# Two scan chains in one pass: the forward states of a bidirectional state-space kernel computed in the projection

## The reference

```python
acum = cumsum(dt * a)                       # per head, inside the chunk
decay = exp(acum[l] - acum[s])              # lower triangle
y_diag = (C @ B.T * decay) @ (x * dt)       # "inside" the chunk
chunk_state = B.T @ (x * dt * exp(acum[-1] - acum))
h_next = h * exp(acum[-1]) + chunk_state    # the chain over the chunks
y_off = (C @ h) * exp(acum)                 # "offset": what the state before the chunk gives
```

## Time and profile before

| | us |
|---|---|
| median of 3 runs (lowest, highest) | 3406.49 (3401.08, 3413.98) |
| span of the profiled execution | 3403.3 |
| TensorE busy over the span | 3177.5 (93%) |
| VectorE, ScalarE, GpSimd busy | 1650.4 (48%), 966.6 (28%), 373.6 (11%) |
| state steps in the projection, first to last sum | 997 to 1143 |
| output stage of the scan, first and last matmul | 1221.5 to 1525 |

### The profile page before, as it was taken

How to read it: one execution, slowest core, us unless ns; L and a number is a source line. 1 busy time by engine, 2 the same in 40 slices (tenths; PEclk the granted TensorE clock), 3 DMA queues, 4 the chain that set the end, 5 groups by cost and what they waited for, 6 DMA issues and landing times. The chain is left out here.

```text
span 3403.3 us, 37747 instructions
## 1 busy us (share of the span) xinstructions
PE 3177.5 (93%) x14940; PEld 2520.6 (74%) x14940; DVE 1650.4 (48%) x1911; ACT 966.6 (28%) x1784; POOL 373.6 (11%) x229
## 2 busy tenths in 40 slices
PE   8999999997999969977999969999999799999898
PEld 8788888876888847766888858888877455555577
DVE  4645543475014249984444443243343555564365
ACT  4422121111210145532222231233223334433310
POOL 0000000000012136652000000000000201000012
PEclk9999999998999989998999979999999699999899
DMA  6122323432226356544333342223123412210242
GB/s 216 42 61 72 107 89 127 149 109 84 88 97 219 109 166 184 180 138 155 111 112 125 115 158 65 89 87 105 56 93 93 102 38 51 62 38 7 93 130 99
DMA packets 211149, 358.99 MB, mean 105 GB/s; under 512 B 22074, under 2 KB 143674, under 8 KB 203093
## 3 DMA queue, kind: packets, MB, share of 16 engines
q1 hardware_dynamic: 187190, 324.46, 29.6%
q10 hardware_dynamic: 16368, 26.36, 2.2%
q0 software_dynamic: 7456, 6.27, 0.9%
HBM read 235.09 MB, written 121.81 MB: 105 GB/s over the span
## 5 line engine op out<-in xcount | busy, mean ns | idle before, releaser
L668 PE MATMUL p_ps<-hmT_hi,p_w_hi 128*128 128x512 f32 x1312 | 524.1, 399 | 16.4 <-ACT p_work L372 14.1
L668 PE MATMUL p_ps<-hmT_lo,p_w_hi 128*128 128x512 f32 x1312 | 512.8, 391 | 0.0
L668 PE MATMUL p_ps<-hmT_hi,p_w_lo 128*128 128x512 f32 x1280 | 500.9, 391 | 0.0
L1795 PE MATMUL p_ps<-h2T_hi,p_w_hi 128*128 128x512 f32 x800 | 329.3, 412 | 22.1 <-DVE h2T_lo L1652 22.1
L1795 PE MATMUL p_ps<-h2T_lo,p_w_hi 128*128 128x512 f32 x800 | 315.7, 395 | 0.0
L668 PEld LDWEIGHTS p_ps<-hmT_hi,p_w_hi 128*128 128x128 f32 x1312 | 247.8, 189 | 71.4 <-issue 18.6
L1795 PE MATMUL p_ps<-h2T_hi,p_w_lo 128*128 128x512 f32 x768 | 300.4, 391 | 0.0
L668 PEld LDWEIGHTS p_ps<-hmT_lo,p_w_hi 128*128 128x128 f32 x1312 | 248.0, 189 | 49.8
L668 PEld LDWEIGHTS p_ps<-hmT_hi,p_w_lo 128*128 128x128 f32 x1280 | 241.5, 189 | 52.0
L1957 PE MATMUL t_psO<-t_prob,t_v 128*65 128x512 f32 (+3 forms) x640 | 261.1, 530 | 0.9
L2014 ACT ACTIVATE t_prob<-t_psS 128x1024 f32<-128x1024 f32 (+1 forms) x160 | 150.0, 938 | 307.4 <-PE t_psS L1945 178.4
(11 more groups left out here) (382 smaller groups left out, 5812.3 us busy)
## 6 DMA issues: line engine op xcount, KB each, us to landing
p_w_raw<-in_w_in SPq DMA_DIRECT2D x66, 512.0 KB, 6.0
p_spare<-in_wada ACTq DMA_DIRECT2D x32, 512.0 KB, 5.6
p_spare<-scratch_xs_tok SPq DMA_DIRECT2D x19, 512.0 KB, 4.4
scratch_xs_tok<-p_work SPq DMA_DIRECT2D x8, 1152.0 KB, 6.1
p_work<-in_wada SPq DMA_DIRECT2D x16, 512.0 KB, 4.7
p_work<-in_x SPq DMA_DIRECT2D x16, 512.0 KB, 3.6
scratch_dT<-p_work SPq DMA_DIRECT2D x8, 1024.0 KB, 6.0
scratch_zpT<-p_work SPq DMA_DIRECT2D x8, 1024.0 KB, 4.0
```

What stands on the lines that cost most here:

```text
L668: mm = pe.matmul(PS[:, c, 0:width], wt[n][:, q, :], xx[:, q, cols], start=(q == 0 and j == 0), stop=(q == KT - 1 and j == len(terms) - 1))
L1795: mm = pe.matmul(ps[:, c, :], wt[n][:, q, :], xx[:, q, c * CH:(c + 1) * CH], start=(q == 0 and j == 0), stop=(q == KT - 1 and j == len(ter ...
```

## The change

The forward chain moves into the projection. `STEPS` now holds the two context chunks forward, the same two backward, and then a forward and a backward step in turn, 34 in all, one in each slot from (32, 1) to (40, 2). Each direction has one state buffer, updated in place; the first step of each direction copies the sum instead of clearing the state and adding. All forward states go to HBM (`h_fwd` becomes 16 chunks), and the tables `wst` and `cdec` no longer do. The output stage loads `hf` by chunk as it does `hb`; `weighted`, `sums` and `state` are gone there with their loads of `b_tok` and tables. The banks of `psS` become an accumulator for the forward offset, so that each offset waits only for the reading of its own predecessor.

```diff
-    STEPS = [(LT, 0), (LT + 1, 0)] + [(c, 1) for c in range(LT + 1, 0, -1)]
-    step_slot = lambda j: (ZS + (4 + j) // 4, (4 + j) % 4)
+    STEPS = [(LT, 0), (LT + 1, 0), (LT + 1, 1), (LT, 1)] + [x for c in range(LT - 1) for x in ((c, 0), (LT - 1 - c, 1))]
+    step_slot = lambda j: (ZP + 7 + (1 + j) // 4, (1 + j) % 4)
+    def stored(j):
+        return j == 1 or j >= 3
...
-                    if dst is not None:
+                    if stored(j):
+                        dst = a["h_bwd"][c - 1] if d == 1 else a["h_fwd"][c + 1 if c < LT else 0]
                         sp.wait_ge(S["state"], j + 1)
-                        sp.dma_start(dst, state[1 - j % 2]).then_inc(h_out[j % 2], 16)
+                        sp.dma_start(dst, state[d]).then_inc(h_out[d], 16)
+                def pass_states(b):
+                    for c in range(4):
+                        j = steps_at.get((b, c))
+                        if j is not None:
+                            store_state(j)
+                            if j + 2 < len(STEPS):
+                                load_state(j + 2)
...
                     if b == ZP + 7:
                         sp.wait_ge(S["wst_ready"], 1)
-                        sp.dma_start(a["ssd_rows"][2], wst).then_inc(S["dec_out"], 16)
-                        sp.dma_start(a["ssd_rows"][3], cdec).then_inc(S["dec_out"], 16)
-                        sp.wait_ge(S["dec_out"], 64)
+                        sp.wait_ge(S["dec_out"], 32)
                         load_state(0)
                         load_state(1)
+                        pass_states(b)
...
                 def advance(j):
                     c, d = STEPS[j]
+                    banks = state[d].rearrange("p (b c) -> p b c", b=2)
+                    if j in (0, 2):
+                        v.wait_ge(S["summed"], j + 1)
+                        v.tensor_copy(banks, PS[:, 6:8, :]).then_inc(S["state"], 1)
+                        v.wait_ge(S["state"], j + 1)
+                        return
...
-                    step(v.tensor_tensor(by_head(new), by_head(old), decay, ALU.mult))
+                    step(v.tensor_tensor(by_head(state[d]), by_head(state[d]), decay, ALU.mult))
                     v.wait_ge(S["summed"], j + 1)
-                    v.tensor_tensor(new.rearrange("p (b c) -> p b c", b=2), new.rearrange("p (b c) -> p b c", b=2), PS[:, 6:8, :],
-                                    ALU.add).then_inc(S["state"], 1)
+                    v.tensor_tensor(banks, banks, PS[:, 6:8, :], ALU.add).then_inc(S["state"], 1)
```

In `ssd`, SP issues `load_hf(c + 2)` behind the load of `z` and a wait for the forward offset of c; VectorE and TensorE become:

```diff
-        psS, psY, psO = (kit.psum(ctx, n, [P, W_HALF]) for n in ("psSt", "psY", "psO"))
+        psF, psY, psO = (kit.psum(ctx, n, [P, W_HALF]) for n in ("psForward", "psY", "psO"))
...
-                    if c + 2 < NC - 1:
-                        sp.wait_ge(S["summed"], c + 1)
-                        load_bt(c + 2)
...
                     if c + 2 < NC:
+                        sp.wait_ge(S["off_f"], c + 1)
+                        load_hf(c + 2)
                         sp.wait_ge(S["inside"], c + 1)
                         load_xs(c + 2)
...
-                    if c + 1 < NC - 1:
-                        weighted(c + 1)
...
                 for c in range(NC):
                     if c < NC - 1:
-                        state(c)
                         decays(c + 1)
                     forward(c)
                     backward(c)
...
                     if c >= 1:
-                        pe.wait_ge(S["state"], c)
-                        pe.wait_ge(S["off_b_read"], c)
-                    offset(c, hf[c % 2]).then_inc(S["off_f"], 1)
+                        pe.wait_ge(S["off_f_read"], c)
+                    pe.wait_ge(f_in[c % 2], 16 * (c // 2 + 1))
+                    offset(c, psF, hf[c % 2]).then_inc(S["off_f"], 1)
...
-                    pe.wait_ge(S["off_f_read"], c + 1)
+                    if c >= 1:
+                        pe.wait_ge(S["off_b_read"], c)
                     pe.wait_ge(h_in[c % 2], 16 * (c // 2 + 1))
-                    offset(c, hb[c % 2]).then_inc(S["off_b"], 1)
-                    if c + 1 < NC - 1:
-                        sums(c + 1)
+                    offset(c, psO, hb[c % 2]).then_inc(S["off_b"], 1)
```

More of the change, by code:

```diff
@@ L113, in tile_cols @@
         return slice(t * P, (t + 1) * P) if t < LT else slice(CTX_AT + (t - LT) * P, CTX_AT + (t - LT + 1) * P)
-    STEPS = [(LT, 0), (LT + 1, 0)] + [(c, 1) for c in range(LT + 1, 0, -1)]
-    step_slot = lambda j: (ZS + (4 + j) // 4, (4 + j) % 4)
+    STEPS = [(LT, 0), (LT + 1, 0), (LT + 1, 1), (LT, 1)] + [x for c in range(LT - 1) for x in ((c, 0), (LT - 1 - c, 1))]
+    step_slot = lambda j: (ZP + 7 + (1 + j) // 4, (1 + j) % 4)
     steps_at = {step_slot(j): j for j in range(len(STEPS))}
+    def stored(j):
+        return j == 1 or j >= 3
     def stored_before(j):
-        return sum(m == 1 or m >= 3 for m in range(j % 2, j, 2))
+        return sum(stored(m) and STEPS[m][1] == STEPS[j][1] for m in range(j))
     half_at = {(UU + j // 4, j % 4): j for j in range(32)}
@@ L258, in _ @@
                         store_act(b - 1)
[L259 to L265, removed]
+                    if b > ZP + 7:
+                        pass_states(b)
                     if b >= 1:
@@ L603, in _ @@
                 for b in range(NB):
[L604 to L608, removed]
+                    if 1 <= b < ZS:
+                        read_groups(b - 1, range(5))
+                    for c in range(4):
+                        if b >= ZS:
                             read_groups(b - 1, (c,))
-                            if (b, c) in steps_at:
-                                advance(steps_at[b, c])
+                        if (b, c) in steps_at:
+                            advance(steps_at[b, c])
                     if b < DT:
@@ L766, in ssd @@
         some = lambda name, count, shape: [sb(f"{name}{n}", shape) for n in range(count)]
-        lndt, eac, wst, cdec = (sb("y_" + n, [P, LT, NDH]) for n in ("lndt", "eac", "wst", "cdec"))
+        lndt, eac = (sb("y_" + n, [P, LT, NDH]) for n in ("lndt", "eac"))
         dskip = sb("y_dskip", [P, HEADS])
@@ L780, in ssd @@
         psCB = psE[:, 1]
-        psS, psY, psO = (kit.psum(ctx, n, [P, W_HALF]) for n in ("psSt", "psY", "psO"))
+        psF, psY, psO = (kit.psum(ctx, n, [P, W_HALF]) for n in ("psForward", "psY", "psO"))
         k = kit
-        S = k.sems("y_", ("cb", "cb_copied", "weighted", "summed", "state", "seg", "exp", "skip",
+        S = k.sems("y_", ("cb", "cb_copied", "seg", "exp", "skip",
                           "merged", "decays", "inside", "off_f", "off_f_read", "forward", "off_b", "off_b_read", "summed_y",
@@ L786, in ssd @@
                           "w_lo"))
-        bT_in, bt_in, x_in, h_in, y_out = ([k.sem(f"y_{what}{n}") for n in range(2)] for what in
-                                           ("bT_loaded", "b_loaded", "xs_loaded", "hb_loaded", "stored"))
+        bT_in, f_in, x_in, h_in, y_out = ([k.sem(f"y_{what}{n}") for n in range(2)] for what in
+                                          ("bT_loaded", "hf_loaded", "xs_loaded", "hb_loaded", "stored"))
         cT_in = [k.sem(f"y_cT_loaded{n}") for n in range(4)]
@@ L800, in load_cT, with load_hf @@
                     sp.dma_start(cT[c % 4][:], cols(a["cT"], c)).then_inc(cT_in[c % 4], 16)
-                def load_bt(c):
-                    sp.dma_start(bt[c % 2][:], tokens(a["b_tok"], c)).then_inc(bt_in[c % 2], 16)
+                def load_hf(c):
+                    sp.dma_start(hf[c % 2][:], a["h_fwd"][c]).then_inc(f_in[c % 2], 16)
                 def load_xs(c):
@@ L854, in _ @@
             def _(g):
[L855 to L860, removed]
                 def skip(c):
@@ L879, in _ @@
                 load_rows(0)
-                g.wait_ge(S["rows_in"], 80)
-                weighted(0)
+                g.wait_ge(S["rows_in"], 32)
                 skip(0)
@@ L947, in step @@
                     v.wait_ge(dve.sem, dve.value)
[L948 to L956, removed]
                 def decays(c):
@@ L968, in forward @@
                         v.wait_ge(y_out[c % 2], 16 * (c // 2))
-                    v.tensor_tensor(by_head(y[c % 2][:]), by_head(psO[:]), heads_of(part(eac, c, 0)),
+                    v.tensor_tensor(by_head(y[c % 2][:]), by_head(psF[:]), heads_of(part(eac, c, 0)),
                                     ALU.mult).then_inc(S["off_f_read"], 1)
@@ L1024, in exponents, with offset @@
                               stop=True).then_inc(S["seg"], 1)
[L1025 to L1028, removed]
-                        pe.wait_ge(S["state"], c)
-                    for g in range(GROUPS):
[L1031 to L1036, removed]
+                def offset(c, to, state):
+                    for g in range(GROUPS):
+                        mm = pe.matmul(to[:, g * 256:(g + 1) * 256], cT[c % 4][:, g, :], state[:, g * 256:(g + 1) * 256],
                                        start=True, stop=True)
```

35 lines of the change are left out of this document (12 added, 23 removed).

## The result

The change makes the kernel slower: 3427.07 us in the median of five runs (3421.66 to 3432.82), where the kernel before took 3406.49 in five runs beside them (3400.21 to 3413.98). The ratio is 1.0058, with a 95% interval of 1.0041 to 1.0076. That is outside the predicted range (3364 to 3400), and on the figure of the third rival, 3427. The profiled execution took 3425.35 us, its span is 3423.5.

The account below looks back on a forecast made before the run. It took TensorE and VectorE waiting for each other to bound the output stage, and TensorE the projection. Projection 29.5 us slower, output stage 58.0 faster (47.5 + 9.2 + 1.3), sum -28.5: from 3406.5 to 3378 us, range 3364 to 3400.

Parts of the forecast that it names:

- the third rival: Output stage: segment rows late in every chunk, TensorE slowed behind the wait, 18.1 us a chunk, 3427 us; chance 0.07.
- the segment rows: Output stage: small GpSimd loads issued after skip, landing in 3.1 us median; 0.4 us of waiting a chunk, bounds 0 and 2.3.
- The point of need: Output stage: TensorE asks for the segment rows 6.3 us after skip's start, where it asked at 8.8 before.
- the tail and the start: Output stage: the last two chunks gain 9.2 us, and the first chunk starts 1.3 us sooner.
- The projection: Projection stage: 15 added steps, block ends and start make it 25.7 + 3.3 + 0.5 = 29.5 us slower.
- The six block ends: Projection: late sums where blocks end; four cost 6.7 us before, two more add 3.3, bounds 1.8 and 17.3.
- the start cost nothing: Projection: the chain starting at block 32 instead of 34 was charged 0.5 us, bounds 0 to 3.
- The output stage's floor: Output stage: 13.76 us of chunk work plus 0.15 for ScalarE's signal, before any wait for segment rows.
- VectorE's work: Output stage: VectorE falls from 16.5 to 12.5 us busy a chunk, under the 13.9, so not the bound.
- The accumulator's wait: Output stage: the backward offset's wait for VectorE to read the shared accumulator, 15.8 us in all, goes.
- The last two chunks: Output stage's end: last forward offset needs only its predecessor's reading, at 1506.9; 9.2 us gained, bounds 4.0 and 11.
- The beginning of the stage: Output stage's first chunk: 0.79 MB of loads fall away ahead of its constants; 1.3 us gained, bounds 0 and 2.6.

Follow-up runs that it names:

- e3: The changed kernel with SP holding the loads of hb, bT and cT until the segment rows have landed; 3380.15 us, ratio 0.9927 to the kernel before.
- e1: The changed kernel with GpSimd issuing the segment rows of chunk c + 3 ahead of skip(c + 1); 3385.13 us, ratio 0.9942 to the kernel before.
- e9: The changed kernel with eight extra unread matmuls where TensorE would wait for the segment rows; 3407.59 us, ratio 0.9997 to the kernel before.
- e2: The changed kernel without segment row loads after chunk 2 and without TensorE's wait for them; 3375.01 us, ratio 0.9914 to the kernel before.
- e4: The changed kernel's output stage on the projection of the kernel before, without the 15 added steps; 3399.04 us, ratio 0.9978 to the kernel before.

## Why the prediction was wrong

**The step that failed** is the segment rows: "Between landing never late (0) and always at 5.6 (2.3) I take 0.4, near the median." The point of need was right: counted at 6.3 us after skip's start, 6.4 in the chunk shown. The time at which the rows are there was wrong, twice. First, the 3.1 us of the earlier trace rows is the median over both `seg_l` pieces of a chunk, while TensorE waits for the last one, and the 3.0 us of issue that the sum adds are those of the last one. Its own median before was 4.1: 3.0 + 4.1 is 0.8 us past the point of need even with nothing changed around it. Second, the landing was kept although the sum itself had moved what surrounds it. The wait of the backward offset that the change removes had also held back SP's 512 KB load; without it the bulk follows the first row piece in 0.4 us instead of a median of 1.5, and the last piece lands in 5.4. That is 8.4 against 6.3, and the wait measured 2.1 us, not 0.4. e3 shows that the bulk is decisive: with it held, the pieces land in 2.4 us in the median and the same late issue costs next to nothing. That the spacing of 1.5 alone would have kept the landing at 4.1 was not tested in the changed kernel; in e1, with 1.46 but with the `xs` load 1.05 us nearer ahead, the median over both pieces was still 4.3.

**Its price was mis-sized with it.** The forecast charged 0.4 for waiting and nothing for the clock. For a wait so short nothing is right: in e1 some 0.7 at a time left the clock at 1.00. The prediction had read in the earlier trace rows that a wait of 2.1 us cost 4.0, and used it for the rival alone. e9 shows that the same holds here: 2.1 us of standing and 1.7 of slower matmuls, 17.72 against 13.87. In the rival the figures were 2.3 and 1.9 on 13.9.

**The rival that came true** did so in its outcome: e1, e2 and e3, which remove the late rows in three ways, show that they and the clock behind them are what cost the gain. Its reason for the longer landing, that all transfers of a chunk go in less time, is not what the runs show: e3 moves 242 GB/s, more than the changed kernel's 195, and the pieces land in 2.4 us. That the total hit its 3427 is partly luck: the chunks took 4.9 us less than it counted, while the tail and the start brought 3.9 and 3.2 less. Its chance of 0.07 was too low.

**The Trainium skill on this.** The trace shows SP's 512 KB load issued 0.4 us behind GpSimd's first row piece, and the 16 KB pieces landing in 4.8 us instead of the 2.4 of e3. The Trainium skill (DMA: Bandwidth & Descriptors, Issuing engines are not separate DMA queues) says that transfers started by either engine run on the same 16 DMA engines and interleave; e3 agrees. The estimate from the page's figures that the prediction weighed, 2.04 us for such a piece, is near the least that e3 shows (2.2) and under half of the median in the changed kernel.

**What held.** The projection: +29.1 for +29.5, with slots of 7.19 and 7.64, and e4 puts 28 on it. The six block ends cost 8.6 us over slots of 7.64 (3.8 of it at the last one), where 6.7 + 3.3 = 10.0 was counted; the start cost nothing, for 0.5. The output stage's floor: 13.87 in e2 for 13.76 + 0.15. VectorE's work: 11.9 us a chunk, under the 12.5 counted, so it never was the bound. The accumulator's wait is gone.

**What was smaller.** The last two chunks gave 5.3 us of 9.2. The last forward offset followed its predecessor's reading at once, as predicted, but that reading came late on VectorE. The first of the two decay operations ahead of it was stretched, with GpSimd at work beside it: 4.44 us for the 2.29 that the same one took before. The second took 3.87 in both. The offset behind them ran at the lower clock, 3.48 us for 1.89.

```profile
1526.96 4.44 DVE L938 TENSOR_TENSOR y_decay_f<-y_decay_f,y_decay_b 128x2048 f32<-128x2048 f32 x1
1531.43 3.87 DVE L942 TENSOR_TENSOR y_decay_f<-y_decay_f,y_cb 128x2048 f32<-128x2048 f32 x1
...
1536.50 2.76 PEld L1007 LDWEIGHTS psForward<-y_hf,y_cT 128*128 128x128 f32 x8 [4.83 <-DVE y_out L948]
```

The same operation in the kernel before:

```profile
1503.57 2.29 DVE L959 TENSOR_TENSOR y_decay_f<-y_decay_f,y_decay_b 128x2048 f32<-128x2048 f32 x1
```

The beginning of the stage lost 1.9 us where 1.3 of gain was counted. There the products of chunk 1 ran at the lower clock, 2.04 us for the 1.05 that the same ones took before. First the kernel before, then the changed one:

```profile
1236.17 1.05 PE L1012 MATMUL psSeg<-y_cT,y_bT 128*128 128x128 f32 x8
```
```profile
1265.28 2.04 PE L992 MATMUL psSeg<-y_cT,y_bT 128*128 128x128 f32 x8 [1.32 <-ACT y_decay_b L910]
```

The granted clock was 1.00 from 1240 on in the kernel before; here it was still 0.54 from 1270 to 1278. The state sum that had stood ahead of these products is gone, and TensorE has less to do between the waits for ScalarE. That this is what lowered the clock there was not tested and stays a reading.

## What to carry to other kernels

When a change shortens a loop, take each small transfer that is needed late in it and work out two things anew: how long from its issue to its need, and what bulk load is now released beside it; a wait that is removed may have been what kept them apart. Where several pieces are needed, take the landing of the last one and not a median over all. Issue the small urgent transfer first, or hold the bulk until it has landed. In this kernel a wait of TensorE near 2 us cost nearly twice its length, at a block end and in every chunk, and one of 0.7 us only itself: look at the granted clock before looking for a second cause.

## What the runs showed of the hardware

In the 13 chunks the granted clock fell behind waits of TensorE near 2 us and not behind those of 0.7. 2.1 us of standing in one piece per 17.72 us chunk gave a mean of 0.89; some 0.7 at a time in 14.56 (e1) gave 1.00, as did the nearly full stretch of e9. The total of the standing differs too (12% and 5% of the time), so these runs do not tell the length of a wait from its share. Eight useless matmuls a chunk made the kernel some 20 us faster.

How long a small transfer takes is not read from how busy the DMA engines are in the mean. The share was 0.72 in e3, where the 16 KB pieces landed in 2.4 us, and 0.61 in the changed kernel, where they took 4.8 beside the bulk. Only the landing times of the tile show it.
